# The first two projection chunks made in token halves, with the input turned in two groups of four blocks

## What is computed

```
h = rms_norm(x, pre_norm[0])          # x * rsqrt(mean(x*x) + eps) * g
proj = h @ w_in                       # 1024 x 2304
q, k, v, ga, u, gb = split(proj)
```

## Time and profile before

| | us |
|---|---|
| median of 3 runs | 2035.73 (2032.13 to 2036.91) |
| the profiled execution | 2034.13 |
| its span in the trace | 2032.3 |
| TensorE busy | 1947.0 |
| VectorE, GpSimd, ScalarE busy | 1300.5, 1139.9, 725.4 |
| mean granted clock of TensorE, as a share of full speed | 0.985 |

### The profile page before, as it was taken

One profiled execution on the slowest core, in us unless ns is written; L12 is line 12 of the kernel. 1 busy time (PEld: TensorE's weight loads), 2 busy tenths in 40 slices (PEclk: granted clock), 3 DMA queues, 4 the chain that ended last, 5 costly groups with the idle time before them and its releaser, 6 DMA issues.

```text
span 2032.3 us, 24978 instructions
## 1 busy us (share of the span) xinstructions
PE 1947.0 (96%) x9212; PEld 1563.5 (77%) x9212; DVE 1300.5 (64%) x1852; ACT 725.4 (36%) x1209; POOL 1139.9 (56%) x936
## 2 busy tenths in 40 slices
PE   7999999999999999899999899999999999999997
PEld 6887877887777788778887565687788887888885
DVE  6127563679997996351673477467544447777778
ACT  3002653442245542330210455324322324545542
POOL 3221115569988995435542100127877878988885
PEclk9999999999999999999999899999999999999999
DMA  5431117455544554438523543335657668676652
GB/s 192 144 120 69 42 42 254 170 182 182 178 168 156 172 181 146 165 133 247 179 85 94 125 86 74 134 136 175 214 195 233 219 206 311 217 257 210 216 189 101
DMA packets 104504, 335.43 MB, mean 165 GB/s; under 512 B 12672, under 2 KB 12928, under 8 KB 103616
## 3 DMA queue, kind: packets, MB, share of 16 engines
q1 hardware_dynamic: 55616, 192.74, 29.4%
q0 software_dynamic: 30384, 106.44, 15.4%
q10 hardware_dynamic: 18384, 34.66, 4.6%
HBM read 272.75 MB, written 46.20 MB: 157 GB/s over the span
## 4 chain that ended last, share of the span: by engine, by line
PE 42%; issue 31%; POOL 21%; DVE 4%; DMA 1%; ACT 1%; POOLq 0%; ACTq 0%; DVEq 0%
PE PS L1215 28%; PE PS L1760 12%; POOL WL L983 12%; POOL RBM L1022 3%; POOL SQH L1022 2%; POOL WH L976 2%; DMA WH<-weights 1%; DVE ACC L3274 1%; DVE ACC L3295 1%; DVE OT L3349 0%; PE PS L1669 0%; DVE PS L2662 0%; DVE PS L2682 0%; POOL G L1024 0%; DVE OPL L3250 0%
## 5 line engine op out<-in xcount | busy, mean ns | idle before, releaser
L1215 PE MATMUL PS<-XHM,WH 128*128 128x512 f32 (+2 forms) x1464 | 524.1, 382 | 24.7 <-POOL WL L983 11.6
L1215 PE MATMUL PS<-XLM,WH 128*128 128x512 f32 (+2 forms) x1464 | 511.0, 373 | 0.0
L1215 PE MATMUL PS<-XHM,WL 128*128 128x512 f32 (+2 forms) x1464 | 510.9, 373 | 0.0
L976 POOL DMA_DIRECT2D WH<-weights x149 | 85.6, 574 | 704.5 <-PE PS L1215 687.6
L983 POOL TENSOR_TENSOR WL<-WRAW,WH 128x1024 fp32r<-128x1024 f32 x149 | 362.2, 2431 | 34.3 <-DMA WH<-weights 22.0
L1215 PEld LDWEIGHTS PS<-XHM,WH 128*128 128x128 f32 x1464 | 271.3, 190 | 86.5 <-POOL WL L983 17.9
L1215 PEld LDWEIGHTS PS<-XLM,WH 128*128 128x128 f32 x1464 | 277.8, 190 | 49.8 <-issue 1.7
L1215 PEld LDWEIGHTS PS<-XHM,WL 128*128 128x128 f32 x1464 | 277.2, 189 | 48.8
L2713 DVE SCALAR_TENSOR_TENSOR PS<-G,TAPW,PS 128x512 f32<-128x512 f32 x319 | 215.8, 753 | 0.6
L3274 DVE TENSOR_TENSOR ACC<-ACC,PS 128x1024 f32<-128x1024 f32 (+1 forms) x113 | 119.8, 1073 | 15.8 <-PE PS L1215 12.9
L1215 PE MATMUL PS<-OPH,VSH 128*128 128x512 f32 x256 | 99.9, 390 | 2.8 <-issue 2.5
(11 more groups left out here) (381 smaller groups left out, 3973.8 us busy)
## 6 DMA issues: line engine op xcount, KB each, us to landing
WRAW<-weights SPq DMA_DIRECT2D x211, 512.0 KB, 3.5
WH<-weights POOLq DMA_DIRECT2D x195, 512.0 KB, 4.5
OPR<-inner SPq DMA_DIRECT2D x56, 512.0 KB, 6.6
inner<-STAGE ACTq DMA_DIRECT2D x56, 256.0 KB, 4.3
inner<-TOUT ACTq DMA_DIRECT2D x48, 256.0 KB, 4.5
XTOK<-x SPq DMA_DIRECT2D x8, 512.0 KB, 7.7
x_kept<-X SPq DMA_DIRECT2D x4, 1024.0 KB, 7.1
X<-x_kept SPq DMA_DIRECT2D x8, 512.0 KB, 5.0
```

What stands on the lines that cost most here:

```text
L976: g.dma_start(WH[:, u, :], weights[WORDER[p]]).then_inc(w_hi[u], 16)
L1215: m = nc.tensor.matmul(dst[:, a:b], w, v[:, a:b], start=first and n == 0, stop=last and n == 2)
```

## The change

Six things change, all ahead of chunk 2.

- SyncE issues the raw weights of chunk 0 first, then the eight input blocks, then the raw weights of chunks 1 and 2 without waiting for the last block.
- GpSimd issues the high weights of chunk 0 as soon as the identity is made. After its constants it subtracts chunk 0's weights, waits for input block 5, and issues those of chunks 1 and 2. The subtraction for chunk 2 waits for all lows of the second token half too.
- TensorE makes eight matmuls on the identity, turns blocks 0 to 3, makes chunk 0 for tokens 0 to 511, turns blocks 4 to 7, and then makes chunk 1 for the first half and chunks 0 and 1 for the second. Blocks rotate over three PSUM slots (`x_slot`) that leave banks 0 and 1 to chunk 0.
- VectorE copies the even blocks out, ScalarE the odd ones (`turned_in`; `x_turned` counts ScalarE's). VectorE counts two for each on `evacuated`.
- Highs and lows are made per half of 512 tokens (`first_hi`, `first_lo`), with semaphores `x0_hi` and `x0_split` for the first half, and the old ones for the second.
- The squares follow the highs of the second half, in the old form.

```diff
+        def x_slot(b):
+            return bank((4, 6, 2)[b % 3], 2)
@@ SyncE
-            for b in range(NB):
-                sp.dma_start(XTOK[:, b, :], x[b * P:(b + 1) * P, :]).then_inc(x_in[b], 16)
             load(0)
-            sp.wait_ge(x_in[NB - 1], 16)
+            for b in range(NB):
+                sp.dma_start(XTOK[:, b, :], x[b * P:(b + 1) * P, :]).then_inc(x_in[b], 16)
@@ GpSimd, low(p)
+                if p == 2:
+                    pool.wait_ge(x_split, X_IN0 + KD)
@@ GpSimd, after IDENT is made
+            high(0)
@@ GpSimd
-            for p in range(P_END):
+            low(0)
+            pool.wait_ge(x_in[NB - 3], 16)
+            high(1)
+            for p in range(2, P_END):
                 high(p)
-                if p >= 1:
-                    low(p - 1)
+                low(p - 1)
@@ TensorE
+            def warm_up():
+                pe.wait_ge(consts, 2)
+                for n in range(8):
+                    nc.tensor.matmul(bank(7)[:, 0:P], IDENT[:], IDENT[:], start=True, stop=True)
+            def transpose_in(b):
+                if b >= 3:
+                    if b % 2:
+                        pe.wait_ge(evacuated, b - 1)
+                    else:
+                        pe.wait_ge(x_turned, (b - 2) // 2)
+                pe.wait_ge(x_in[b], 16)
+                for k in range(KD):
+                    last = nc.tensor.transpose(x_slot(b)[:, k * P:(k + 1) * P], XTOK[:, b, k * P:(k + 1) * P], IDENT[:])
+                full.by(last)
+            def first_half(p, h):
+                pe.wait_ge(w_ready, p + 1)
+                if p == 1 and h == 0:
+                    pe.wait_ge(x_turned, 3)
+                for k in range(KD):
+                    pe.wait_ge(x_split if h else x0_split, k + 1)
+                    m = three(slot0(p)[:, tokens(h)], WH[:, p, k * P:(k + 1) * P], WL[:, p, k * P:(k + 1) * P],
+                              XH[:, k, tokens(h)], XL[:, k, tokens(h)], k == 0, k == KD - 1, ((0, HALF),))
+                if h:
+                    m.then_inc(psum_full, 1)
@@
-            transposes_in()
-            for c in range(14):
+            warm_up()
+            for b in range(4):
+                transpose_in(b)
+            first_half(0, 0)
+            for b in range(4, NB):
+                transpose_in(b)
+            first_half(1, 0)
+            first_half(0, 1)
+            first_half(1, 1)
+            for c in range(2, 14):
@@ ScalarE
-            act.wait_ge(evacuated, NB)
-            for k in range(KD):
-                hi(k, X[:, k, :], G_PRE0)
+            def turned_in(b):
+                act.wait_ge(psum_full, b + 1)
+                nc.scalar.activation(X[:, :, b * P:(b + 1) * P], x_slot(b).rearrange("p (k t) -> p k t", k=KD),
+                                     ACT.Copy).then_inc(x_turned, 1)
+            def first_hi(h, k):
+                nc.scalar.activation(XH[:, k, tokens(h)], X[:, k, tokens(h)], ACT.Copy,
+                                     scale=GAINS[:, G_PRE0, k:k + 1]).then_inc(x_hi if h else x0_hi, 1)
+            for h in range(2):
+                for b in range(4 * h + 1, 4 * h + 4, 2):
+                    turned_in(b)
+                act.wait_ge(x_turned, 2 * h + 2)
+                act.wait_ge(evacuated, 4 * h + 4)
+                for k in range(KD):
+                    first_hi(h, k)
@@ VectorE
-            for b in range(NB):
-                dve.wait_ge(psum_full, b + 1)
-                v.tensor_copy(X[:, :, b * P:(b + 1) * P], slot(b).rearrange("p (k t) -> p k t", k=KD)).then_inc(evacuated, 1)
-            dve.wait_ge(evacuated, NB)
-            for k in range(KD):
-                lo(X_IN0, k, X[:, k, :], G_PRE0)
+            for h in range(2):
+                for b in range(4 * h, 4 * h + 4, 2):
+                    turned_in(b)
+                dve.wait_ge(x_turned, 2 * h + 2)
+                dve.wait_ge(evacuated, 4 * h + 4)
+                for k in range(KD):
+                    first_lo(h, k)
```

More of the change, by code:

```diff
@@ L391, in sem @@
             return ctx.enter_context(nc.semaphore(name))
+        x_turned = sem("x_turned")
+        x0_hi = sem("x0_hi")
+        x0_split = sem("x0_split")
         x_in = [sem(f"x_in{b}") for b in range(NB)]
@@ L947, in _, with high, low @@
                                   pattern=[[-1, P]], channel_multiplier=1))
+            def high(p):
+                u = p % NW
+                if p >= NW:
+                    pool.wait_ge(*W_DONE[p - NW])
+                g.dma_start(WH[:, u, :], weights[WORDER[p]]).then_inc(w_hi[u], 16)
+            def low(p):
+                u, n = p % NW, p // NW + 1
+                pool.wait_ge(w_in[u], 16 * n)
+                pool.wait_ge(w_hi[u], 16 * n)
+                if p == 2:
+                    pool.wait_ge(x_split, X_IN0 + KD)
+                g.tensor_tensor(WL[:, u, :], WRAW[:, u, :], WH[:, u, :].bitcast(F32), ALU.subtract)\
+                    .then_inc(w_ready, 1)
+            high(0)
             const(g.memset(COLSEL[:], 0.0))
@@ L969, in _ @@
                                   pattern=[[1, 2 * P]], channel_multiplier=-1))
[L971 to L984, removed]
             inited = Signal(sem_init)
@@ L1874, in _ @@
             nc.scalar.activation(SMALL[:, 94:95], GAINS[:, G_PRE0, 0:1], ACT.Copy, scale=GAINS[:, G_PRE0, 0:1])
-            def hi(k, src, gain):
-                nc.scalar.activation(XH[:, k, :], src, ACT.Copy, scale=GAINS[:, gain, k:k + 1]).then_inc(x_hi, 1)
             def half_hi(h, k, src):
@@ L2470, in then @@
                 dve.wait_ge(step.sem, step.by(ins))
[L2472 to L2476, removed]
             def half_lo(h, x_ready, k, src):
@@ L2519, in take, with turned_in, first_lo @@
                 dve.wait_ge(evacuated, use + 1)
-            for b in range(NB):
+            def turned_in(b):
                 dve.wait_ge(psum_full, b + 1)
-                v.tensor_copy(X[:, :, b * P:(b + 1) * P], slot(b).rearrange("p (k t) -> p k t", k=KD)).then_inc(evacuated, 1)
-            dve.wait_ge(evacuated, NB)
-            for k in range(KD):
-                lo(X_IN0, k, X[:, k, :], G_PRE0)
+                v.tensor_copy(X[:, :, b * P:(b + 1) * P], x_slot(b).rearrange("p (k t) -> p k t", k=KD))\
+                    .then_inc(evacuated, 2)
+            def first_lo(h, k):
+                dve.wait_ge(x_hi if h else x0_hi, k + 1)
+                v.scalar_tensor_tensor(out=XL[:, k, tokens(h)], in0=X[:, k, tokens(h)], scalar=GAINS[:, G_PRE0, k:k + 1],
+                                       in1=XH[:, k, tokens(h)].bitcast(F32), op0=ALU.mult,
+                                       op1=ALU.subtract).then_inc(x_split if h else x0_split, 1)
+            for h in range(2):
[5 more added lines that the diff above has]
+                    first_lo(h, k)
             for k in range(KD):
```

5 lines of the change are left out of this document (removed).

## The result

The changed kernel takes 2039.90 us as the median of 13 executions (2035.40 to 2045.28), the kernel before 2034.75 beside it (13, 2031.64 to 2039.77): a ratio of 1.0025, interval 1.0015 to 1.0036. The change makes the kernel slower by 0.15 to 0.25%, 3 to 5 us.

The account below looks back on a forecast made before the run. TensorE, busy 96% of the span, was taken as the bound, so the row sum's time decides: row sum +2.0 us and clock +1.0 on a median of 2035.73 gave 2038.7 us, range 2034.6 to 2041.6.

Parts of the forecast that it names:

- Loads: Opening transfers: input up to 2.6 us later, ScalarE's small loads 1.3 us later, so ScalarE free at 14.25.
- First half product: TensorE's chunk 0 for tokens 0 to 511: start 17.9, 5.45 us of work plus 1.6 at lower clock, end 25.0.
- Rival 1: Chunk 1's subtraction lands among first-half lows: product ends 26.2, mark moves 3.2, total +4.9 us, 2040.6; chance 0.25.
- Chunk 2 and TensorE's arrival: After transposes of 4.25 us and three half products of 16.3, chunk 2 starts at 45.6; TensorE reaches the mark at 49.65.
- The chain: The norm's squares and VectorE's seven additions: start 37.5, sum ready at 52.85, TensorE waits 3.2 us for it.
- the second hold: Chunk 3's GpSimd subtraction also holds a VectorE addition in the norm: between 0 and 2.75 us, taken as 2.4.
- the mark: TensorE's row sum of squares in mid chunk 2, at 50.82 before the change; forecast 2.0 us later.
- Clock: TensorE's lower clock after its wait for the row sum: a loss of 0 to 1.7 us, taken as 1.0.
- Sum: Total shift of the kernel: mark +2.0 and clock +1.0 give +3.0 us, a median of 2038.7.
- carry the difference to the end: Code behind the row sum is unchanged, so the opening's shift was taken to reach the kernel's end unaltered.
- I would be wrong if the total moved by more than the mark and the clock do: Sign against the forecast, over the whole kernel: such a movement would mean that a later stage feels the shift.
- within 0.2%: Outcome for the whole kernel's time: no change beyond about 4.1 us, the measurement's resolution; chance 0.67.

Follow-up runs that it names:

- loads_only: The kernel before with only the changed order of the load transfers; ratio 1.0000 to the kernel before.
- no_hold_low1: Changed kernel with GpSimd's subtractions for chunks 1 and 2 behind the first half's lows, chunk 3's behind the sixth addition; ratio 0.9998 to the kernel before.
- before_more_hold: The kernel before with one extra GpSimd subtraction on dead data behind chunk 2's; ratio 0.9997 to the kernel before.
- all_of_it: Changed kernel with ScalarE first awaiting only its gains, and GpSimd's subtractions moved out of first-half lows and norm additions; ratio 0.9977 to the kernel before.
- all_of_it_again: all_of_it repeated unaltered for more executions; ratio 0.9995 to the kernel before.

## Why the prediction was right, and where it was not

The forecast was 2038.7 us with a range of 2034.6 to 2041.6; the time is 2039.9. The closeness is partly luck: the forecast stood on a median of 2035.73 for the kernel before, which was 2034.75 beside the change, so that a shift of 3.0 was forecast and 5.15 was measured. The mechanism in the opening was the one forecast: the early start is given back at the row sum, because the norm's chain starts later and GpSimd holds VectorE in it twice. Step by step:

- *Loads.* ScalarE free at 14.25 forecast, 14.13 measured; the small loads were 1.28 us later, for 1.3. The load order alone makes 0.97 of that (loads_only). The bound that the input comes up to 2.6 later held for its middle (block 4 at 13.51 in loads_only, for 13.8 forecast), not for its end (0.32).
- *First half product.* Start 17.9, measured 17.85. Its end 25.0, measured 25.54: it ran 7.69 us, of which 5.45 were the work and 2.2 the clock, at the upper end of my 0.8 to 2.4. The 1.6 taken in between was too small; the lower level held from the first matmul on in both traces of the change.
- *Rival 1's hold.* It happened: chunk 1's subtraction at 21.08 fell among the first half's lows, which took 7.52 instead of 5.39. But it didn't cost its 1.2 us. TensorE, at the lower clock, was slower than the lows. no_hold_low1 took the hold away and didn't end the product sooner (26.29).
- *Chunk 2 and TensorE's arrival.* 45.6 and 49.65 forecast, 45.37 and 49.61 measured (51.96 less 2.35). The 0.5 us lost above came back in the transposes: 3.41 from start to start (25.54 to 28.95) instead of 4.25, since the 1.06 of a row is a length that holds the pipeline. The three half products took 16.42, for 16.3.
- *The chain.* Start 37.5, measured 37.24. Length 15.36, measured 14.57: the second hold was 2.0, not 2.4, and the first 0.4 shorter than that of the earlier trace rows. So the sum was ready at 51.81 instead of 52.85, the wait was 2.35 instead of 3.2, and the mark moved by 1.14 (1.29 in the second trace), not 2.0.
- *Clock.* 1.0 taken between 0 and 1.7; it was 1.6 in one trace (2.73 less 1.14) and 0 in the other. Both ends occurred, after waits of 2.35 and 2.36. Over the five traces with a wait of 2.35 or more, the spreading matmul follows the row sum by 7.48 to 7.77 us in four and by 6.14, as without a wait, in one: the clock cost 1.3 to 1.6 in four and nothing in the fifth. The stretch read in the earlier trace rows begins 1.28 us behind the restart at 820.62, not with it.
- *Sum.* The opening was forecast 3.0 late; 2.73 and 1.29 were measured. Mark too large and clock too small nearly cancelled in the first trace.

The step that failed is the last one, "carry the difference to the end". That the profiled execution ended 2.79 us behind, near the forecast 3.0, is luck: the same trace was 0.94 ahead at 1099 us. I had written that I would be wrong if the total moved by more than the mark and the clock do. By the two ratios it moved 4 to 5 us, 2 to 3 more than the two openings; by the pooled means 3.6, about 1.6 more than their mean of 2.0. My reading of that sign, that a later stage feels the shift, isn't shown: loads_only drifts as much with hardly a shift, and the means of the versions with halves lie above the shift even where it is negative. Part of the rest could be chance in the executions drawn, part the opening of the kernel before, known from few traces, and that stays open. The case that I held likeliest, within 0.2%, was missed narrowly: both ratios are at or above 1.0020, to which I gave 0.29.

## What to carry to other kernels

When work is started earlier, look for the chain off the path whose start moves the other way and for the releases on other engines that move closer together; here two subtractions that had been 11 us apart came 5.4 apart and both landed in the same chain. Cost a hold by whether anybody waits for the held engine: one hold cost 2 to 2.5 us of the opening in the changed kernel and nothing that could be measured in the kernel before. And judge a change of 0.2% by some twenty executions, since two executions of the same code lay up to 9.9 us apart here (2035.40 and 2045.28).

## What was not expected of the hardware

- *An operation of VectorE can be held by a subtraction that starts later.* In before_more_hold VectorE's low started at 20.80, half a microsecond ahead of the subtraction at 21.30, but within GpSimd's issue from 20.70 to 21.27, and was held until 24.76, 1.1 us after the subtraction's end. The Trainium skill's page "SBUF — State Buffer", section "Who interferes with whom", lets the order of issue decide which of the two blocks; this row would agree if GpSimd's DMA issue counted as its turn. But that doesn't cover all rows either. In the changed kernel this addition started 0.08 us behind the issue at 45.84 and was not held, while the subtraction behind it took 2.98 instead of 2.41:

```profile
45.92 1.23 DVE L2543 TENSOR_TENSOR SSUM<-SSUM,SQ 128x1024 f32<-128x1024 f32 x1
```

What decides between the two stays open.

- *The clock after an idle isn't a function of the idle's length.* After 2.86 us (all_of_it) the first half product ran at the full level, after 2.85 (all_of_it_again) its first 2.7 us went at 0.50; after the wait of 2.35 it fell in one trace of the change and not in the other.
